# A third of a modulation product from TensorE matmuls to VectorE row products, and the latent heads' stage reordered

## The chip, the core and the metric

The kernel runs on one core of a Trainium2 chip. The metric is the time of one execution on the device in microseconds; the median of several runs is given. The core has five engines that run their own instruction streams and wait for each other through semaphores: TensorE (PE, matmuls into PSUM), VectorE (DVE), ScalarE (ACT), GpSimd (POOL) and SyncE (SP), which here only starts DMAs.

## What is computed

The reference applies two transformer blocks to 256 tokens of width 1024. The first one has stick-breaking attention and latent (MLA) attention side by side, an output projection, and an up projection, a convolution of three taps, a gate and a down projection. The second one begins with a modulation of its norms by a conditioning vector `c`:

```python
cond = jax.nn.silu(c)                       # (1, 1024)
mod = cond @ mod_w[l] + mod_b[l]            # mod_w: 1024 x 6144
sh1, sc1, g1, sh2, sc2, g2 = jnp.split(mod, 6, axis=-1)
h = _rmsnorm(x, norm1_g[l]) * (1 + sc1) + sh1
z = h @ w_in[l]
```

Everything is float32. `mod` depends on `c` and the weights alone, so the kernel may compute it at any time before the second block. Its first third (`sh1` and `sc1`, 2048 values) is the part that this change touches. The expert layer of the second block, which follows much later, reads most of the weights.

## The kernel before

All tiles have 128 partitions. Each engine has a function that issues its instructions in a fixed order (`tensor`, `scalar`, `vector`, `gpsimd`, `sync`), and every order is written out by hand; signals between the engines are named marks on semaphores. The instructions are recorded by helpers of one line each, so in the profile L107 is any matmul, L110 any transpose, L113 an activation, L116 a copy on ScalarE, L119 a table load, L125 a `tensor_tensor`, L133 a `scalar_tensor_tensor`, L136 a reciprocal.

The weights stream through a ring of seven slots of 2 MB. `STREAM` (line 51) gives the order of the loads and `PLACE` the slot of each; SP issues them in that order, each after the last use (`used`) of what lay in its slot, so a load that has to wait also holds up those behind it.

The modulation weights are twelve ring slots `modw` 0 to 11, four for each third of `mod`. `mod_slot(j)` multiplies one of them on TensorE: eight matmuls whose weights are 128x32 tiles of silu(c) with one column that isn't zero, and whose moving data are 512 columns of the modulation weights (each appears as two in the trace, x16). `mod_half` is half of that. `mod_sum` on VectorE copies the sums out of PSUM, `mod_total` turns them to a column per feature on TensorE and adds the bias on VectorE.

In the latent heads' stage (84 to 111 us) four pairs of heads, i = 0 to 3, go through `mla_scores(i)` on TensorE, `maxima` on VectorE, `shares` on ScalarE (Exp with sums) and on VectorE (division), `turn` on TensorE (six transposes), `turned` on ScalarE (copy out of PSUM), `values` on TensorE. TensorE's order puts `mod_slot` 0 to 5 and half of 6 in between. The same stage holds the root of the group norm for the stick-breaking heads (`column_sums(7, ...)`, `group_sums(0)`, a product for the total, `group_root(0)`, `group_factor(0)`, `group_norm(0..3)`), with the root near the end, and the rounding of the output projection's weights (`out_rounded`, `out_rest`) and inputs (`out_input`).

In the up projection each matmul operand of float32 is split in a high part (rounded by ScalarE, `up_rounded`) and a low part (what is left, by VectorE, or by GpSimd for the keys in `POOL_UP`: k = 3 and 7 of every block j from 1 on). Block j = 0 to 10 has one ring slot of weights and eight steps k with twelve matmuls of 256 columns; four weight buffers are used in turn, so the rounding of step n waits for the matmuls of step n - 4, and TensorE waits for the low part ahead of each step. The convolution, gelu and gating of block j - 1 are spread over the steps of block j (`conv_step`); GpSimd does the gated product and the low part of its result. The down projection does the same over 44 steps i with matmuls of 512 columns, all low parts of its weights on VectorE.

## Time and profile before

| | before |
|---|---|
| median of 3 runs | 939.18 us (938.42 to 939.66) |
| the profiled execution | 939.0 us, of which span 937.3 us |
| mean granted clock of TensorE | 0.937 of full speed |
| busy TensorE / VectorE / ScalarE / GpSimd | 84% / 37% / 33% / 13% of the span |
| DMA | 297.95 MB, mean 318 GB/s |

The profile shows one execution. A row of the timeline merges instructions that follow each other: start in us, time from the first start to the last end in us, engine, line, operation, output and inputs, forms, count, and in brackets the engine's idle time before it and what ended that. PEclk is the clock that TensorE was granted, as a share of full speed. Matmuls are pipelined, so successive groups overlap by a little.

### The profile page before, as it was taken

How to read it: one execution, taken by the hardware profiler on the slowest of the kernel's cores; microseconds unless marked ns; L12 is line 12 of the kernel's file. 1: busy time of each engine (PE TensorE's matmuls, PEld its weight loads, DVE VectorE, ACT ScalarE, POOL GpSimd, SP SyncE). 2: the span in 40 equal slices, each digit the busy share in tenths (PEclk: the TensorE clock that was granted, in tenths of full speed). 3: DMA queues.
4: the chain of work that ended last, by engine and by line, in shares of the span. 5: the costliest groups of instructions: out<-in, count | busy, mean ns of one | idle time of the engine just before them, and what ended most of it. 6: DMA issues, size and time to landing. Idle time of an engine off the chain costs nothing.

```text
span 937.3 us, 12394 instructions
## 1 busy us (share of the span) xinstructions
PE 790.7 (84%) x5204; PEld 524.5 (56%) x5204; DVE 349.4 (37%) x767; ACT 312.4 (33%) x623; POOL 125.7 (13%) x129
## 2 busy tenths in 40 slices
PE   9999999999999999999999998567666566755765
PEld 7985588999998867688786343123221222211213
DVE  6647766777776554399513110010100101001002
ACT  5756655766665476313633010001000000000002
POOL 0011032444441033100211000000000000000000
PEclk9999999999999999999999997988796998979868
DMA  9955917755535475735559999999999999999995
GB/s 357 407 188 216 430 66 299 293 187 189 189 132 186 180 261 199 282 134 191 214 229 408 429 429 427 427 429 426 429 428 428 429 426 430 425 428 430 427 427 208
DMA packets 24111, 297.95 MB, mean 318 GB/s; under 512 B 2672, under 2 KB 3056, under 8 KB 5488
## 3 DMA queue, kind: packets, MB, share of 16 engines
q1 hardware_dynamic: 24048, 297.09, 77.5%
q8 instruction: 43, 0.70, 0.3%
q14 instruction: 20, 0.16, 0.1%
HBM read 296.03 MB, written 1.05 MB: 317 GB/s over the span
## 4 chain that ended last, share of the span: by engine, by line
PE 57%; DMA 33%; ACT 4%; DVE 4%; issue 1%; POOL 0%; DVEq 0%; ACTq 0%; POOLq 0%
PE ps L107 57%; DMA ring<-in_exps 33%; ACT ar L113 1%; ACT ar L116 1%; ACT fr L116 1%; PE ps L110 1%; DVE ar L125 1%; ACT sq L113 0%; DVE fr L125 0%; DVE fr L133 0%; DVE misc L148 0%; DVE xg L133 0%; DVE yT L125 0%; DVE yT L133 0%; ACT L113 0%
## 5 line engine op out<-in xcount | busy, mean ns | idle before, releaser
L107 PE MATMUL ps<-ring,sq 128*32 128x512 f32 x944 | 139.7, 728 | 75.4 <-DMA ring<-in_exps 75.0
L107 PE MATMUL ps<-fr 128*128 128x256 f32 (+1 forms) x956 | 163.2, 323 | 1.9 <-ACT ar L116 1.4
L107 PEld LDWEIGHTS ps<-fr 128*128 128x128 f32 x956 | 140.1, 190 | 17.7 <-ACT ar L116 2.2
L107 PE MATMUL ps<-ring,ar 128*32 128x512 f32 (+3 forms) x792 | 102.4, 601 | 40.8 <-DMA ring<-in_exps 35.0
L107 PEld LDWEIGHTS ps<-ring,sq 128*32 128x32 f32 x944 | 29.1, 122 | 173.3 <-DMA ring<-in_exps 119.7
L125 DVE TENSOR_TENSOR ar<-ar,ps 128x512 f32<-128x512 f32 x9 | 6.2, 687 | 261.3 <-PE ps L107 261.3
L125 DVE TENSOR_TENSOR fr<-ring,fr 128x512 fp32r<-128x512 f32 (+1 forms) x96 | 77.9, 830 | 48.3 <-ACT fr L116 48.0
L116 ACT ACTIVATE ar<-ps 128x512 f32<-128x512 f32 (+4 forms) x48 | 27.2, 570 | 178.5 <-PE ps L110 145.5
L107 PEld LDWEIGHTS ps<-ring,ar 128*32 128x32 f32 (+1 forms) x792 | 27.1, 118 | 96.0 <-DMA ring<-in_exps 53.0
L107 PE MATMUL ps<-ar 128*128 128x512 f32 (+9 forms) x320 | 66.2, 427 | 11.0 <-DVE ar L125 9.3
L116 ACT ACTIVATE fr<-ring 128x512 fp32r<-128x512 f32 (+1 forms) x114 | 66.5, 623 | 25.6 <-PE ps L107 22.5
L107 PE MATMUL ps<-fr,fr_h 128*128 128x256 f32 x528 | 66.9, 283 | 0.0
L107 PEld LDWEIGHTS ps<-fr,fr_h 128*128 128x128 f32 x528 | 64.9, 191 | 0.0
L113 ACT ACTIVATE sq<-ps,misc 128x128 f32<-128x128 f32 x31 | 11.9, 456 | 158.1 <-PE ps L107 158.1
L125 DVE TENSOR_TENSOR ar<-ps,ar 128x512 f32<-128x512 f32 (+5 forms) x36 | 23.0, 659 | 110.6 <-PE ps L107 110.3
L107 PE MATMUL ps<-hT,ring 128*128 128x256 f32 (+1 forms) x288 | 64.0, 383 | 0.3 <-ACT hT L113 0.3
L107 PEld LDWEIGHTS ps<-ar 128*128 128x128 f32 (+4 forms) x320 | 36.3, 173 | 43.7 <-DVE ar L125 20.1
L107 PEld LDWEIGHTS ps<-hT,ring 128*128 128x128 f32 (+1 forms) x288 | 54.3, 190 | 9.8 <-issue 1.5
L125 POOL TENSOR_TENSOR ar<-ar 128x128 f32<-128x128 f32 (+2 forms) x21 | 11.2, 533 | 311.5 <-DVE ar L125 310.4
L113 ACT ACTIVATE ar<-ps 128x768 f32<-128x768 f32 (+1 forms) x21 | 15.0, 716 | 96.6 <-PE ps L107 89.4
L116 ACT ACTIVATE fr_h<-ring 128x512 fp32r<-128x512 f32 x66 | 40.2, 629 | 17.7 <-PE ps L107 17.7
L125 DVE TENSOR_TENSOR fr_h<-ring,fr_h 128x512 fp32r<-128x512 f32 x43 | 30.8, 716 | 25.8 <-ACT fr_h L116 25.8
(188 smaller groups left out, 929.7 us busy)
## 6 DMA issues: line engine op xcount, KB each, us to landing
ring<-in_exps SPq DMA_DIRECT2D x86, 2048.0 KB, 30.9
ring<-in_modw SPq DMA_DIRECT2D x12, 2048.0 KB, 8.8
ring<-in_wup SPq DMA_DIRECT2D x11, 2048.0 KB, 12.2
ring<-in_wdown SPq DMA_DIRECT2D x5, 2048.0 KB, 7.7
ar<-in_exps SPq DMA_DIRECT2D x5, 2048.0 KB, 13.0
ring<-in_win SPq DMA_DIRECT2D x4, 2048.0 KB, 8.2
ring<-in_exps SPq DMA_DIRECT2D x6, 1024.0 KB, 8.7
ring<-in_wo SPq DMA_DIRECT2D x2, 2048.0 KB, 9.7
```

The lines of the kernel that those rows point to most:

```text
L107: return Issue(self.e and self.e.matmul(o, l, r, start=start, stop=stop, skip_group_check=True))
L110: return Issue(self.e and self.e.transpose(o, i, ident))
L113: return Issue(self.e and self.e.activation(o, i, f, **kw))
L116: return Issue(self.e and self.e.activation(o, i, ACT.Copy, scale=scale))
L125: return Issue(self.e and self.e.tensor_tensor(o, a, b, op))
```

## The change

The first third of the modulation leaves TensorE and goes to VectorE. The host lays out `modw` 0 to 3 so that a partition holds a feature's column, 1024 long, and a slot holds 4 such tiles. `c` is loaded as a row into all partitions (`crow`, 512 KB), ScalarE takes its Silu after the first block of the up projection, and 16 instructions `tensor_tensor_reduce` on VectorE (`mod_column`) multiply 1024 elements by that row and sum them to one value of `mod` per partition: ten in the up projection (after the low part of k = 6 of blocks 1 to 10) and six in the down projection (ahead of the low parts of i = 5, 9, 13, 17, 21 and 25). The loads of `modw` 0 to 3 move to among those of the up projection's weights, and the slots of all loads around them change places.

In the latent heads' stage TensorE keeps `modw` 4, 5 and half of 6 between its steps. The root of the stick-breaking group goes from the end of the stage to its beginning, ahead of the first Exp on ScalarE, with a table load ahead of it and one behind it, and the group norms, the inputs and the rounded weights of the output projection are spread between the steps of the softmax.

```diff
-STREAM = ([("win", 1), ("win", 3), ("win", 2), ("wqkv", 0)] + [("modw", j) for j in range(7)] + [("wo", 0), ("wo", 1), ("wup", 0), ("modw", 7)]
-          + [("wup", j) for j in range(1, 11)] + [("wdown", j) for j in range(6)] + [("wple", 0), ("wgate", 0), ("wgate", 1)]
+STREAM = ([("win", 1), ("win", 3), ("win", 2), ("wqkv", 0)] + [("modw", 4), ("modw", 5), ("modw", 6), ("wo", 0), ("wo", 1), ("wup", 0), ("modw", 7)]
+          + [("wup", 1), ("modw", 0), ("wup", 2), ("wup", 3), ("wup", 4), ("modw", 1), ("wup", 5), ("wup", 6), ("wup", 7), ("wup", 8), ("modw", 2)]
+          + [("wup", 9), ("wup", 10), ("modw", 3)] + [("wdown", j) for j in range(6)] + [("wple", 0), ("wgate", 0), ("wgate", 1)]
...
+    def products_sum(self, o, a, b, total):
+        return Issue(self.e and self.e.tensor_tensor_reduce(out=o, in0=a, in1=b, scale=1.0, scalar=0.0, op0=ALU.mult, op1=ALU.add,
+                                                            accum_out=total))
...
             mla_scores(0)
-            mla_scores(1)
-            mod_slot(0, dve_lat["vm", 1])
-            mod_slot(1)
             pe.wait_ge(act_stick["o", 1])
             column_sums(7, [(tile(ar, k), act_stick["osq", k // 2]) for k in range(4)]).then_inc(pe_wo, "sums", 0)
+            mla_scores(1)
+            pe.wait_ge(act_wo["sums", 0])
+            pe.matmul(half(7, 1), ones, sd[:, 0, :], True, True).then_inc(pe_wo, "total", 0)
+            mod_slot(4, dve_lat["vm", 0])
             turn("mla", 0, mla_s[0])
-            mod_slot(2)
             mla_scores(2)
             turn("mla", 1, mla_s[1])
-            mod_slot(3)
-            pe.wait_ge(act_wo["sums", 0])
-            pe.matmul(half(7, 1), ones, sd[:, 0, :], True, True).then_inc(pe_wo, "total", 0)
+            mod_half(5, 0)
             mla_scores(3)
             values("mla", 0, mla_p[0], vm, dve_lat["vm", 1], dve_lat["qm", 3])
             values("mla", 1, mla_p[1], vm)
-            mod_slot(4, dve_lat["vm", 0])
+            mod_half(5, 1)
             turn("mla", 2, mla_s[0])
-            mod_slot(5)
+            mod_half(6, 0)
             turn("mla", 3, mla_s[1])
             values("mla", 2, mla_p[0], vm, act_wo["root", 0])
-            mod_half(6, 0)
             values("mla", 3, mla_p[1], vm)
-            mod_total(0)
...
+            act.tables("sqrt_and_others")
+            group_sums(0)
+            group_root(0)
+            act.tables("exp_and_others")
             shares("mla", 0, mla_s[0], scale)
             shares("mla", 1, mla_s[1], scale)
-            group_sums(0)
             turned("mla", 0, mla_p[0])
             turned("mla", 1, mla_p[1])
+            out_rounded(0, 0)
             shares("mla", 2, mla_s[0], scale)
+            out_input(0)
+            out_input(1)
             shares("mla", 3, mla_s[1], scale)
-            group_root(0)
             turned("mla", 2, mla_p[0])
+            out_input(2)
+            out_input(3)
+            out_rounded(0, 1)
             turned("mla", 3, mla_p[1])
...
+                if j == 0:
+                    act.wait_ge(landed["crow"]["all"])
+                    act.activation(sq[:, 0:1024], sq[:, 0:1024], ACT.Silu).then_inc(act_mod, "crow")
...
+            group_factor(0)
             maxima("mla", 2, mla_s[0], mla_mask, scale)
-            mod_sum(0)
+            for k in range(2):
+                group_norm(k)
             maxima("mla", 3, mla_s[1], mla_mask, scale)
             shares("mla", 2, mla_s[0])
+            for k in range(2, 4):
+                group_norm(k)
             shares("mla", 3, mla_s[1])
-            group_factor(0)
-            for k in range(4):
-                group_norm(k)
...
-            mod_total(0)
...
+            def mod_column(i):
+
+                j, o = i // 4, 1024 * (i % 4)
+                dve.wait_ge(loaded("modw", j), act_mod["crow"])
+                if i > 0:
+                    dve.wait_ge(dve_mod["column", i - 1])
+                t = dve.products_sum(sq[:, 1024:2048], slot("modw", j)[:, o:o + 1024], sq[:, 0:1024], mod[:, i:i + 1]).then_inc(dve_mod, "column", i)
+                if i == 15:
+                    dve.wait_ge(t)
+                    dve.tensor_tensor(mod[:, 0:16], mod[:, 0:16], col("mod_b", 0, 16), ALU.add).then_inc(dve_mod, "mod", 0)
+
+            DOWN_COLUMNS = (5, 9, 13, 17, 21, 25)
...
                     if j:
                         conv_step(j - 1, k)
+                    if j and k == 6:
+                        mod_column(j - 1)
...
+                if i in DOWN_COLUMNS:
+                    mod_column(10 + DOWN_COLUMNS.index(i))
                 dve.wait_ge(act_down["hi", f, n])
...
-                return (pe_mod["slot", j],)
+                return (dve_mod["column", 4 * j + 3] if j < 4 else pe_mod["slot", j],)
...
+                if (name, j) == ("wup", 2):
+                    sp.wait_ge(pe_joint["mix", "sums"])
+                    sp.dma_start(sq[:, 0:1024], A["crow"]).then_inc(landed["crow"], "all")
```

## Rows read from the trace of the kernel before

**Rows 1.** The page's part 4, the chain that ended last, by engine.

```profile
PE 57%; DMA 33%; ACT 4%; DVE 4%; issue 1%; POOL 0%; DVEq 0%; ACTq 0%; POOLq 0%
```

**Rows 2.** Windows: stretch and length, busy us of each engine, PEclk, DMA share, GB/s.

```profile
84.00:117.00 33.00, 31.30 (x246) 16.94 (x243) 23.85 (x55) 21.65 (x58) 1.28 (x1) 1.00 0.97 398
160.00:334.00 174.00, 174.00 (x1221) 163.84 (x1220) 114.08 (x192) 107.31 (x196) 60.88 (x42) 1.00 0.54 200
```

**Rows 3.** Timeline of TensorE in the latent heads' stage (columns as described above).

```profile
87.79 3.64 PE L107 MATMUL ps<-ring,ar 128*32 128x512 f32 x32
...
92.96 1.92 PE L107 MATMUL ps<-ring,ar 128*32 128x512 f32 x16
...
110.35 1.05 PE L107 MATMUL ps<-con,ar 128*128 128x4 f32 x8
111.26 2.11 PE L107 MATMUL ps<-fr 128*128 128x512 f32 x8
```

**Rows 4.** Timeline of ScalarE in the same stage.

```profile
85.71 0.63 ACT L113 ACTIVATE ar<-hT 128x512 f32<-128x512 f32 x1
88.90 0.40 ACT L113 ACTIVATE yT<-yT,misc 128x128 f32<-128x128 f32 x1 [2.56 <-DVE misc L129]
...
105.00 1.28 ACT L113 ACT_TABLE_LOAD   x1
...
107.84 0.81 ACT L116 ACTIVATE sq<-ps 128x768 f32<-128x768 f32 x1 [0.37 <-PE ps L110]
...
117.40 0.47 ACT L113 ACTIVATE sd<-ps,misc 128x256 f32<-128x256 f32 x1 [0.79 <-PE ps L107]
```

**Rows 5.** Timeline of VectorE in the same stage.

```profile
91.09 1.01 DVE L129 TENSOR_SCALAR yT<-yT,misc 128x128 f32<-128x128 f32 x4
...
96.43 0.96 DVE L125 TENSOR_TENSOR yT<-ps,yT 128x768 f32<-128x768 f32 x1 [2.31 <-PE ps L107]
...
106.81 1.75 DVE L136 RECIPROCAL rb<-sd 128x256 f32<-128x256 f32 x1 [0.57 <-ACT sd L113]
...
110.18 0.69 DVE L125 TENSOR_TENSOR fr<-ring,fr 128x512 fp32r<-128x512 f32 x1
```

**Rows 6.** Expert stage: a group of TensorE's timeline, and the window around it.

```profile
571.05 3.64 PE L107 MATMUL ps<-ring,ar 128*32 128x512 f32 x16 [2.97 <-DMA ring<-in_exps]
...
570.00:575.00 5.00, 3.64 (x16) 0.60 (x16) 0.24 (x1) 0.00 (x0) 0.00 (x0) 0.52 0.98 416
```

**Rows 7.** Timeline of VectorE, then of GpSimd, about one turn of the blocks.

```profile
177.97 0.68 DVE L125 TENSOR_TENSOR fr_h<-ring,fr_h 128x512 fp32r<-128x512 f32 x1
181.02 0.70 DVE L125 TENSOR_TENSOR fr<-ring,fr 128x512 fp32r<-128x512 f32 x1 [2.37 <-ACT fr L116]
181.65 1.77 DVE L125 TENSOR_TENSOR fr<-ring,fr 128x512 fp32r<-128x512 f32 x1
...
178.22 1.58 POOL L125 TENSOR_TENSOR yT<-yT 128x512 f32<-128x512 f32 x1 [3.27 <-DVE yT L133]
179.88 1.30 POOL L125 TENSOR_TENSOR fr_h<-ring,fr_h 128x512 fp32r<-128x512 f32 x1
181.26 1.62 POOL L125 TENSOR_TENSOR fr<-yT,fr 128x512 fp32r<-128x512 f32 x1
```

**Rows 8.** The same two engines at the end of the first block.

```profile
154.16 1.43 DVE L125 TENSOR_TENSOR fr_h<-ring,fr_h 128x512 fp32r<-128x512 f32 x1 [0.35 <-ACT fr_h L116]
...
153.75 1.29 POOL L125 TENSOR_TENSOR fr<-ring,fr 128x512 fp32r<-128x512 f32 x1 [12.63 <-ACT fr L116]
155.12 1.62 POOL L125 TENSOR_TENSOR fr_h<-ring,fr_h 128x512 fp32r<-128x512 f32 x1
```

**Rows 9.** Timeline of TensorE in the period of rows 7.

```profile
179.90 3.04 PE L107 MATMUL ps<-fr,fr_h 128*128 128x256 f32 x24
182.77 3.04 PE L107 MATMUL ps<-fr 128*128 128x256 f32 x24
```

**Rows 10.** The page's part 6, DMA issues: count, KB each, median us to landing.

```profile
ring<-in_wgate SPq DMA_DIRECT2D x2, 2048.0 KB, 7.6
```

More of the change, by code:

```diff
@@ L213, in build @@
         landed = {n: Signal(sem(f"{n}_in"), 16) for n in (
-            ["x0", "x2", "x4", "w0", "w1", "w2", "w4", "w6", "cols", "con", "rcount", "k4", "pos", "p", "brow"]
+            ["x0", "x2", "x4", "w0", "w1", "w2", "w4", "w6", "cols", "con", "rcount", "k4", "pos", "p", "brow", "crow"]
             + ["more3", "more6", "more7", "more8", "more9", "again17", "again18", "half0", "half1"])}
@@ L699, in tensor @@
                     if (j, n) == (0, 0):
-                        pe.wait_ge(dve_mod["mod", 0])
+                        pe.wait_ge(dve_lat["vm", 1])
                         column_sums(5, [(tile(sq, k), act_wo["osq", k // 2]) for k in range(4)]).then_inc(pe_wo, "sums", 1)
@@ L1266, in out_rounded @@
                 src, hi, _ = wo_part(n, k)
-                act.wait_ge(loaded("wo", n), pe_soft["mla", "scores", 3])
                 i = WO_ORDER.index((n, k))
+                act.wait_ge(loaded("wo", n), pe_soft["mla", "scores", 3] if i > 1 else pe_stick["values", 3])
                 if i > 7:
@@ L1293, in scalar @@
             scale = 96 ** -0.5
+            act.tables("sqrt_and_others")
+            group_sums(0)
+            group_root(0)
+            act.tables("exp_and_others")
             shares("mla", 0, mla_s[0], scale)
             shares("mla", 1, mla_s[1], scale)
-            group_sums(0)
             turned("mla", 0, mla_p[0])
             turned("mla", 1, mla_p[1])
+            out_rounded(0, 0)
             shares("mla", 2, mla_s[0], scale)
+            out_input(0)
+            out_input(1)
             shares("mla", 3, mla_s[1], scale)
-            group_root(0)
             turned("mla", 2, mla_p[0])
+            out_input(2)
+            out_input(3)
+            out_rounded(0, 1)
             turned("mla", 3, mla_p[1])
-            out_rounded(0, 0)
-            out_rounded(0, 1)
-            for k in range(4):
-                out_input(k)
-                if k == 1:
-                    mla_out(0)
-                elif k > 1:
-                    out_rounded(0, k)
+            out_rounded(0, 2)
+            out_rounded(0, 3)
+            mla_out(0)
             mla_out(1)
@@ L1734, in mod_sum @@
             def mod_sum(s):
-                dve.wait_ge(pe_mod["slot", 4 * s + 2], pe_mod["slot", 4 * s + 3], pe_mod["total", s - 1] if s else None)
+                dve.wait_ge(pe_mod["slot", 4 * s + 2], pe_mod["slot", 4 * s + 3], pe_mod["total", s - 1] if s > 1 else None)
                 dve.tensor_copy(ar[:, modp:modp + 512], bank(4 if s else 5)).then_inc(dve_mod, "sum", s)
@@ L1768, in vector @@
                 shares("mla", i, mla_s[i])
+            group_factor(0)
             maxima("mla", 2, mla_s[0], mla_mask, scale)
-            mod_sum(0)
+            for k in range(2):
+                group_norm(k)
             maxima("mla", 3, mla_s[1], mla_mask, scale)
             shares("mla", 2, mla_s[0])
+            for k in range(2, 4):
+                group_norm(k)
             shares("mla", 3, mla_s[1])
-            group_factor(0)
-            for k in range(4):
-                group_norm(k)
             out_rest(0, 0)
@@ L2280, in ring_load @@
                     return
-                if (name, j) == ("modw", 1):
+                if (name, j) == ("modw", 5):
                     sp.wait_ge(pe_in["q", 7])
@@ L2602, in lay_out @@
     A["wgate"] = _slots([L["w_ple_gate"][:, 0:512], L["w_ple_gate"][:, 512:1024]])
-    A["modw"] = np.stack([_rows(L["mod_w_2"][256 * t:256 * t + 256, 2048 * i:2048 * i + 2048]).reshape(128, SLOT)
-                          for i in range(3) for t in range(4)])
+    A["crow"] = np.broadcast_to(L["c_2"][0].reshape(1, 1024), (128, 1024))
+    w = L["mod_w_2"]
+    A["modw"] = np.stack([w[:, 512 * t:512 * t + 512].reshape(1024, 4, 128).transpose(2, 1, 0).reshape(128, SLOT) for t in range(4)]
+                         + [_rows(w[256 * t:256 * t + 256, 2048 * i:2048 * i + 2048]).reshape(128, SLOT) for i in range(1, 3) for t in range(4)])
     w = L["w_in_2"]
```

## The prediction

> **What bounds the kernel now.** I read the chain that ended last first: TensorE carries 57% of it, and almost all the rest (33%) is waiting for DMA [rows 1], in order of time the expert weights of the last 370 us. The windows then give two different stages around the change. From 84 to 117 us (scores and softmax of the latent heads) TensorE has work nearly always (31.30 us of 33), but much of that work is filler: modulation products that stand between steps of a chain from TensorE to VectorE to ScalarE and back [rows 2]. From 160 us to 334 us (up and down projections) TensorE is busy without a gap, 174.00 of 174.00 us, at a granted clock of 1.00 (2.4 GHz) [rows 2]. The filler in the first stage can go without loss; in the second stage anything that makes TensorE wait is paid in full. The DMA tail starts when compute frees ring slots, so a shift of everything ahead of it should arrive at the end one to one, in either direction.
>
> **Part 1: what leaves TensorE.** Slots 0 to 3 of the modulation weights and one turning product go. On TensorE slots 0 and 1 took 3.64 us together, slot 2 1.92 and slot 3 the same, the turning 1.05 [rows 3]: 8.4 us of queue in 23.5 us (87.8 to 111.3). If TensorE were the bound there, 8.4 us would be gained; if the softmax chain were, nothing. So the chain has to be followed.
>
> Before, ScalarE's square ends at 86.3, its first Exp starts at 88.90, and it ends the last turned copy at 108.65 [rows 4]. After the change it first does the root of the stick-breaking group: a table load (1.28, as the one at 105.00), the copy of the sums, a wait for the total, the root (0.47), and a table load back (1.28) [rows 4]. With the third and fourth product of TensorE in between (sums 0.6, scores 1.4, total 0.7) the root ends near 89.7 and the first Exp starts near 91.0: the chain starts 2.1 us later. From there I add the same durations in the new order. Two pairs' Exps, 1.86 each, end at 94.7; the factors of the first pair (VectorE, reciprocal 0.17 and four products 1.01, [rows 5]) are ready at 94.1, its transposes and the turned copy end at 95.8, the third scores at 97.4, where the maxima that wait for them began at 96.43 before [rows 5]. VectorE meanwhile does the group's reciprocal, 1.75 [rows 5], until 97.7; third maxima to 100.0, two norms, fourth maxima from 100.85 to 103.1, about where they were before, Exps to 105.0, factors to 106.35, transposes to 107.3, turned copy to 108.2, values to 109.1. The output products start there instead of at 111.26 [rows 3]: 2.2 us earlier. ScalarE's queue then holds two roundings, the two head outputs, four roundings and the sums: they end at 114.2 instead of 116.6 (2.4 earlier); the second root now has a table load ahead of it, mostly under the total, and ends at 115.9 instead of 117.9 (2.0 earlier), and the low parts that VectorE makes from 119.7 on follow it. **I take 2.2 us gained**; the other 6.2 us of removed products become waits. The two ends are 0 (a wait in my chain missed) and 8.4.
>
> TensorE will idle for about 3 us near 91 to 94. In the expert stage a pause of 2.97 us was followed by a granted clock of 0.52, and 16 products took 3.64 us there instead of 1.92 [rows 6]; other pauses of the same length left the clock at 1.00. If it falls in the latent stage it costs up to about 2 us of the gain.
>
> **Part 2: what VectorE takes up.** Sixteen products with sums, each 128x1024 in and out. No row shows this operation. Products of 512 elements took 0.69 us and of 768 took 0.96 [rows 5], so a kilo-element at the same rate takes 0.96 + 256 x 1.05 ns = 1.23 us. Ends: 1.23 us if the sum is free, about 2.3 us if each element takes twice as long. Sixteen are 20 us of VectorE, which is busy for 114 of 174 us in the two projections [rows 2], so there is room in total. What matters is where they stand.
>
> In each of j = 1 to 10 the column comes after the low part of k = 6. In the period that I read, this low part runs from 177.97 to 178.65, then VectorE is idle for 2.37 us until 181.02 [rows 7]. By VectorE's own queue a column of 1.23 us fits. But GpSimd works in just that gap: the gated product (178.22, 1.58 us), the low part of k = 7 (179.88, 1.30, to 181.18), the low part of the product (181.26, 1.62) [rows 7]. And the two engines keep each other out when both read two operands of SBUF. VectorE's low part at 181.65 took 1.77 us instead of 0.69: it ended 0.54 after GpSimd's instruction of 181.26 did. GpSimd's at 181.26 took 1.62 instead of 1.30, being behind VectorE's of 181.02. The pair at 154.16 and 155.12 shows who is next: VectorE, waiting for GpSimd's 153.75 to end at 155.04, got in ahead of GpSimd's next one, which took 1.62, 0.33 more than alone [rows 8]. The Trainium skill says the same in "SBUF — State Buffer", section "Who interferes with whom": a VectorE instruction with two SBUF inputs and a GpSimd one that reads SBUF exclude each other for the whole instruction. The rows above agree with it.
>
> So the column, issued at about 178.6 behind GpSimd's gated product, will start when that ends (179.8), ahead of the low part of k = 7. That one is then held for 0.33 us (what a VectorE product of 512 cost it) plus 512 more elements, 0.53: 0.86 us. When does TensorE need it? The group of 24 products for k = 6 and 7 starts at 179.90 and the next at 182.77 [rows 9], so k = 7 starts at 181.34, only 0.16 us after 181.18. Part of that is the signal's way between the engines; I take 0.10 us of cover. **Each column stalls TensorE by about 0.76 us, ten times 7.6 us.** It doesn't add up within a period (the low parts of the next block's k = 0 and 1, done at 182.6 and 184.3, are needed at 183.5 and 185.0), nor is it made up for, since each period hangs on TensorE's own progress. If GpSimd got in first the column would start at 181.2 and hold back GpSimd's next one, and with it the low part of k = 0, for a stall of a little over 1 us instead: no order is free.
>
> In the down projection the six columns have no GpSimd work that TensorE needs soon (its last two instructions are wanted at f = 20). A low part is made as soon as a buffer is free, three steps of 1.36 us ahead of its use less 1.4 us of rounding: 2.7 us of cover against a column of 1.23. I take 0; if the cover were gone it would be 1.2 us a column.
>
> **Part 3: ScalarE, ring and queues.** The Silu over 1024 elements costs about 1.0 us (a copy of 768 took 0.81) and a table load 1.28 [rows 4]. It stands ahead of the rounding of (1, 0), whose low part is ready 2.4 us before its use; so 1.3 us of delay is hidden: 0. The row of c goes behind slot 2 of the up weights on SP's queue, which waits for the second half of modulation slot 6; half a megabyte behind two lands some 8 us later, ahead of the Silu. The tightest load is the last up slot: it waits for column 7 (j = 8, k = 6), about 0.9 us after TensorE begins that k; it is wanted a period later, 11.7 us on. Loads of 2 MB with nothing ahead of them landed in 7.6 us [rows 10], and nothing is ahead here: 4 us of cover, so I take 0. Modulation slot 3 and the first down slot stand behind it, 5 us each, and have 3.5 us of cover.
>
> **Sum.** 10 x 0.76 - 2.2 = +5.4 us on the profiled execution (939.0 us, span 937.3), which stands 0.2 under the median of 939.18: 944.6.
>
> **Rivals.** (a) The columns are hidden: the sum form doesn't hold GpSimd back, or TensorE's cover is larger than read. For it: 2.37 us of idle VectorE each period. Against it: [rows 8]. Then only the latent stage counts: 939.2 - 2.2 = 937.0, between 934.5 and 939. Chance 0.20, of it 0.12 beyond the bound of change. (b) The product with sum runs at half rate. Then the lock is held 1.07 us longer, 10 x 1.83 = 18.3, less 2.2: 955.3. This is the far slow side, decided by the duration of one instruction, from about 1.5 us upward. Chance 0.12. The Trainium skill, "Vector Engine (DVE) Microarchitecture Reference", "Points that are easy to get wrong", says a scalar_tensor_tensor with two 32-bit SBUF sources has half the rate with accumulation; no run here shows one yet. (c) The latent stage gives back 5 to 8 us, because the order by hand shortens waits I count as fixed; with the stalls this gives 936.5 to 942, say 939. Chance 0.12, of it 0.05 faster. (d) The forecast, with 0.5 to 1.1 us a column and 0 to 4 us of gain, a fallen clock or a late slot included: 941.2 to 949. Chance 0.56.
>
> A measurement of this kernel can tell 0.2% (1.9 us) from no change. Faster: 0.12 + 0.05 = 0.17. Same: 0.08 + 0.07 = 0.15. Slower: 0.56 + 0.12 = 0.68. The range leaves out (b) and the lower part of (a): 936.5 to 950.
>
> **What would show it.** Right: in each of ten periods a VectorE instruction of 128x1024 that starts inside a GpSimd instruction and is stretched, GpSimd's low part into fr_h at about 2.1 us instead of 1.30, and TensorE waiting some 0.8 us for it; periods of 12.3 us instead of 11.5; six columns of 1.23 us in the down projection with no wait of TensorE; output products beginning near 109 with a pause near 91 to 94. Wrong: periods of 11.5 us (rival a), columns of over 2 us there (b), output products starting before 106 (c), TensorE waiting for the ring in the up projection.

## The result and the profile after

The changed kernel takes 949.74 us (median of 4 runs, 948.91 to 949.97) against 938.80 us (4 runs, 938.31 to 939.66) for the one before on the same chip: 1.0113 of its time, 95% interval 1.0098 to 1.0128. It is **10.9 us slower**. I had forecast slower, with 944.6 us (5.4 us over the profiled run) and a range of 936.5 to 950. The profiled execution of after took 949.59 us, span 947.9, mean granted clock 0.938; that of before 939.0, 937.3 and 0.937.

The page of after first: its part 4 (the chain that ended last, by engine), and two groups of its part 5 (form, count, busy time and mean ns, idle time before and what ended it).

```profile
PE 46%; DMA 33%; DVE 9%; ACT 6%; POOL 4%; issue 1%; SPq 0%; POOLq 0%; DVEq 0%; ACTq 0%
...
L108 PE MATMUL ps<-fr 128*128 128x256 f32 (+1 forms) x956 | 163.2, 323 | 1.6 <-ACT ar L117 1.4
...
L108 PE MATMUL ps<-fr,fr_h 128*128 128x256 f32 x528 | 69.5, 285 | 8.3 <-POOL fr_h L126 8.3
```

Against [rows 1] TensorE has fallen from 57% of the chain to 46%, GpSimd has come from 0 to 4%, VectorE from 4 to 9%. The last row says where: TensorE waits 8.3 us for `fr_h`, the low parts that GpSimd makes.

The same events in both timelines show how the difference grows (starts in us):

| event | before | after | difference |
|---|---|---|---|
| last product ahead of the latent stage (four matmuls behind a ScalarE copy) | 79.95 | 79.29 | -0.66 |
| first transpose behind the output projection | 136.42 | 135.83 | -0.59 |
| up projection, k = 0 of j = 1 | 159.72 | 159.13 | -0.59 |
| first step of the down projection | 274.85 | 285.18 | +10.33 |
| work behind the down projection | 334.72 | 345.05 | +10.33 |
| end of the span | 937.3 | 947.9 | +10.6 |

The first 0.66 us lies ahead of everything that TensorE does differently; in the traces of all kernels of this document that event starts anywhere from 78.86 to 79.97. The latent heads' stage, the work of part 1, comes to +0.07 us where I had -2.2. The ten blocks of the up projection cost **10.92 us** where I had 7.6; the down projection costs nothing, as forecast.

**One period of the up projection**, j = 2, read as [rows 7] and [rows 9]: timelines of VectorE, GpSimd and TensorE of after (start, length, instruction, idle time before it).

```profile
178.21 0.68 DVE L126 TENSOR_TENSOR fr_h<-ring,fr_h 128x512 fp32r<-128x512 f32 x1
178.81 1.22 DVE L156 CUSTOM_DVE_ANT_0 sq<-ring,sq 128x1024 f32<-128x1024 f32 x1
179.96 0.08 DVE L156 DVE_READ_ACCUMULATOR2_ANT misc<- 128x1 f32 x1
...
178.46 2.72 POOL L126 TENSOR_TENSOR yT<-yT 128x512 f32<-128x512 f32 x1 [3.25 <-DVE yT L134]
181.26 1.28 POOL L126 TENSOR_TENSOR fr_h<-ring,fr_h 128x512 fp32r<-128x512 f32 x1
182.61 1.63 POOL L126 TENSOR_TENSOR fr<-yT,fr 128x512 fp32r<-128x512 f32 x1
...
180.13 1.60 PE L108 MATMUL ps<-fr,fr_h 128*128 128x256 f32 x12
182.59 1.70 PE L108 MATMUL ps<-fr,fr_h 128*128 128x256 f32 x12 [0.85 <-POOL fr_h L126]
184.13 3.04 PE L108 MATMUL ps<-fr 128*128 128x256 f32 x24
```

The column (the instruction CUSTOM_DVE_ANT_0 of L156) takes 1.22 us and is not stretched. What is stretched is GpSimd's gated product: 2.72 us against 1.58 in [rows 7], 1.14 more, nearly the whole column. Its next instruction, the low part of k = 7, has its normal 1.28 us but ends 1.13 us later against TensorE's k = 6 than before, and TensorE waits 0.85 us. The steps of k = 6 and k = 7, one group of 24 products before, are now two of 12, and from k = 6 to the next k = 0 it takes 4.00 us (180.13 to 184.13) instead of 2.87. The next period's k = 6 starts at 192.77, 12.64 us later; before, a period was 11.51. All blocks j = 2 to 10 look so (gated product 2.71 or 2.72 us nine times).

In the first period, j = 1, it goes another way (VectorE, GpSimd, TensorE again):

```profile
166.46 2.32 DVE L156 CUSTOM_DVE_ANT_0 sq<-ring,sq 128x1024 f32<-128x1024 f32 x1
...
166.10 1.60 POOL L126 TENSOR_TENSOR yT<-yT 128x512 f32<-128x512 f32 x1 [3.26 <-DVE yT L134]
167.77 2.14 POOL L126 TENSOR_TENSOR fr_h<-ring,fr_h 128x512 fp32r<-128x512 f32 x1
...
167.77 1.60 PE L108 MATMUL ps<-fr,fr_h 128*128 128x256 f32 x12
169.96 1.69 PE L108 MATMUL ps<-fr,fr_h 128*128 128x256 f32 x12 [0.60 <-POOL fr_h L126]
```

Here the column is the one that is held (2.32 us), and it gets in between GpSimd's two instructions, so that the low part takes 2.14 instead of 1.30. That is the picture that I had forecast for all ten, and it costs 12.36 - 11.51 = 0.85 us. With nine of 1.12 to 1.13 that makes the 10.9.

**The latent heads' stage**: TensorE's timeline and the windows (stretch, length, busy us of each engine, granted clock, DMA share, GB/s) of after.

```profile
93.40 1.54 PE L111 MATMUL ps<-con,yT 128*128 128x128 f32 x6 [3.14 <-DVE yT L130]
95.84 2.93 PE L108 MATMUL ps<-ar 96*128 96x128 f32 x8 [0.90 <-ACT ar L117]
98.56 1.49 PE L111 MATMUL ps<-con,yT 128*128 128x128 f32 x6
...
110.67 3.02 PE L108 MATMUL ps<-fr 128*128 128x512 f32 x12
...
94.00:97.00 3.00, 2.10 (x9) 1.61 (x8) 2.72 (x6) 0.81 (x1) 0.00 (x0) 0.50 0.92 393
97.00:100.00 3.00, 3.00 (x16) 2.29 (x14) 1.16 (x2) 0.00 (x0) 0.00 (x0) 0.50 0.01 5
100.00:104.00 4.00, 4.00 (x33) 2.45 (x32) 3.07 (x7) 3.69 (x12) 0.00 (x0) 0.97 0.02 4
```

TensorE idles for 3.14 us behind its filler, and the granted clock is 0.50 (1.2 GHz) in all six microseconds after that: the first transposes take 1.54 us, the third scores 2.93. On the full clock these two take 0.88 and 1.58 us (a row of d2 and one of c1, below). The output projection begins at 110.67.

### The profile page after: what moved, and what is told of

The parts are those of the page before. It is cut to its first block, busy times and chain, and to the rows that moved or that the text cites. A ratio compares the mean times of both kernels' runs of the same rounds, so it can differ in the third digit from the quotient of the medians.

```text
span 947.9 us, 12289 instructions
## 1 busy us (share of the span) xinstructions
PE 783.5 (83%) x5132; PEld 522.7 (55%) x5132; DVE 368.5 (39%) x798; ACT 317.3 (33%) x627; POOL 137.2 (14%) x129
## 4 chain that ended last, share of the span: by engine, by line
PE 46%; DMA 33%; DVE 9%; ACT 6%; POOL 4%; issue 1%; SPq 0%; POOLq 0%; DVEq 0%; ACTq 0%
PE ps L108 45%; DMA ring<-in_exps 32%; DVE yT L134 4%; POOL yT L126 3%; DVE fr L126 2%; POOL fr_h L126 1%; ACT yT L114 1%; ACT ar L114 1%; ACT ar L117 1%; ACT fr L117 1%; DVE fr_h L126 1%; DVE ar L126 1%; DMA ring<-in_win 1%; PE ps L111 1%; ACT fr_h L117 1%
## 5 line engine op out<-in xcount | busy, mean ns | idle before, releaser
L108 PE MATMUL ps<-ring,sq 128*32 128x512 f32 x944 | 136.4, 713 | 78.7 <-DMA ring<-in_exps 78.3
L108 PE MATMUL ps<-ring,ar 128*32 128x512 f32 (+3 forms) x728 | 96.2, 609 | 42.1 <-DMA ring<-in_exps 36.9
L108 PE MATMUL ps<-fr,fr_h 128*128 128x256 f32 x528 | 69.5, 285 | 8.3 <-POOL fr_h L126 8.3
L108 PEld LDWEIGHTS ps<-ar,yT 128*128 128x128 f32 x256 | 32.0, 199 | 15.7 <-issue 14.5
```

The costliest lines, as they stand in the source:

```text
L108: return Issue(self.e and self.e.matmul(o, l, r, start=start, stop=stop, skip_group_check=True))
```

## The experiments

My theory after this reading: (1) all of the loss is the columns of the up projection, because VectorE and GpSimd exclude each other; (2) the gain of the latent stage is there, but the granted clock takes it back. The rival of (1) was a cost of each column that has nothing to do with GpSimd (a fixed price of the new instruction, or its place in VectorE's queue). The rival of (2) was that moving the root ahead of the first Exp costs what the removed products give.

### The columns taken away: a1

```diff
-                t = dve.products_sum(sq[:, 1024:2048], slot("modw", j)[:, o:o + 1024], sq[:, 0:1024], mod[:, i:i + 1]).then_inc(dve_mod, "column", i)
+                t = dve.memset(small[:, 0:1], 0.0).then_inc(dve_mod, "column", i)
...
-                    dve.tensor_tensor(mod[:, 0:16], mod[:, 0:16], col("mod_b", 0, 16), ALU.add).then_inc(dve_mod, "mod", 0)
+                    dve.tensor_copy(mod[:, 0:16], col("mod_b", 0, 16)).then_inc(dve_mod, "mod", 0)
```

> The changed kernel with the sixteen products with sums left out (a memset of one element stands in each one's place, so the signals that free the ring slots stay; the first third of the modulation is then only its bias). Loads, Silu, the order of the latent stage and everything else as in the changed kernel. Theory L (the columns lock GpSimd out of its reads, and nothing else of them costs): periods of the up projection back to 11.51 us from 12.63, so 11.0 us less than the changed kernel: 938.7 us, that is level with the kernel before, since the latent stage gained nothing. Rival W (part of the 11 us is from the loads in their new order, the Silu or the ring): some periods stay longer than 11.51 and the time lies above 940.

Measured: 938.33 us (10 runs), 0.9995 of before (0.9983 to 1.0007; before on this chip 938.39). The whole loss goes with the columns, and what is left of the change (the ring, the row of c, the Silu and the latent stage together) is worth nothing that can be measured: 1.6 us less to 0.7 us more by the interval.

### The columns in another place: a2

```diff
-                    if j and k == 6:
+                    if j and k == 1:
                         mod_column(j - 1)
```

> The same ten columns, each after the low part of k = 1 instead of k = 6. There VectorE has 1.12 us of idle time and GpSimd has nothing until about 2.2 us later. Theory L: VectorE does the same work, but GpSimd's low part of k = 7 is in time again: periods of 11.5 to 11.6 us, 939 us in all (938.5 to 940.5). Rival V (the columns cost because VectorE's queue is too full, so its own low parts come late): the low part of k = 2, which has only some 0.4 us of cover, comes 0.1 us late at most by VectorE's rows, but if V holds the periods stay at 12.3 or more, 947 to 950 us.

Measured: 938.70 us (10 runs), 0.9998 (0.9985 to 1.0010). The window of the up projection, VectorE's column with the low part behind it, and GpSimd's instruction ahead of it, in the trace of a2:

```profile
160.00:285.00 125.00, 125.00 (x1006) 123.37 (x1005) 99.19 (x176) 81.65 (x153) 58.13 (x40) 1.00 0.53 217
...
183.83 1.21 DVE L156 CUSTOM_DVE_ANT_0 sq<-ring,sq 128x1024 f32<-128x1024 f32 x1
184.98 0.08 DVE L156 DVE_READ_ACCUMULATOR2_ANT misc<- 128x1 f32 x1
185.03 0.69 DVE L126 TENSOR_TENSOR fr_h<-ring,fr_h 128x512 fp32r<-128x512 f32 x1
...
181.74 1.62 POOL L126 TENSOR_TENSOR fr<-yT,fr 128x512 fp32r<-128x512 f32 x1
```

All sixteen columns are done, and TensorE is busy for 125.00 of 125.00 us again. GpSimd has just ended when the column starts (its last instruction runs from 181.74 to 183.36, its next one starts at 185.66). So the work itself has no price; its place had one. This is also rival (a) of the prediction, had the change put the columns here.

### Half the length: a3

```diff
-                t = dve.products_sum(sq[:, 1024:2048], slot("modw", j)[:, o:o + 1024], sq[:, 0:1024], mod[:, i:i + 1]).then_inc(dve_mod, "column", i)
+                t = dve.products_sum(sq[:, 1024:1536], slot("modw", j)[:, o:o + 512], sq[:, 0:512], mod[:, i:i + 1]).then_inc(dve_mod, "column", i)
```

> The sixteen products over 512 instead of 1024 elements, in the places of the changed kernel (half of each sum is left out). Theory L with the order seen in the trace (the column goes ahead of GpSimd's gated product and holds it for its whole length): the hold falls by 512 elements of 1.04 ns, from 1.14 to 0.61 us, and the period from 12.63 to 12.10: 5.3 us less over ten periods, 944.4 us. If the stall had a fixed part per instruction (a queue or a drain), the period would stay above 12.3 and the time above 946.5.

Measured: 945.26 us (5 runs), 1.0064 (1.0040 to 1.0088), 6.9 us over before. VectorE and GpSimd in j = 2 of a3:

```profile
178.53 0.68 DVE L156 CUSTOM_DVE_ANT_0 sq<-ring,sq 128x512 f32<-128x512 f32 x1
...
178.18 2.18 POOL L126 TENSOR_TENSOR yT<-yT 128x512 f32<-128x512 f32 x1 [3.27 <-DVE yT L134]
```

The gated product is 0.60 us longer than in [rows 7], against 1.14 with the full column, and the period is 12.11 us, 0.60 over before. Both times that is 0.08 us less than the column takes, 0.68 and 1.22. So the price follows the length of the column (0.53 us less a period for 0.54 us less of column), and no fixed part shows. The first period goes its own way here too: GpSimd's gated product goes first, and j = 1 is only 0.33 us over before (168.01 to 179.85, 11.84 us). With nine of 0.60 that makes 5.7 us, which is what the trace has for the ten blocks (120.80 us from 159.37 to 280.17, 115.13 before); the rest to the 6.9 measured lies within the interval (4 to 8 us).

### One of the two inputs in PSUM: a4

The Silu's row is copied to two banks of PSUM that are free during the up projection, and the ten columns there read it from PSUM; place and length stay. TensorE waits for the last of them before it uses these banks, in the down projection.

```diff
+                        act.copy(ps[:, 6:8, :].rearrange("p b t -> p (b t)"), sq[:, 0:1024]).then_inc(act_mod, "crow")
...
+                row = ps[:, 6:8, :].rearrange("p b t -> p (b t)") if i < 10 else sq[:, 0:1024]
+                t = dve.products_sum(sq[:, 1024:2048], slot("modw", j)[:, o:o + 1024], row, mod[:, i:i + 1]).then_inc(dve_mod, "column", i)
```

> Columns at k = 6 as in the changed kernel and as long, but for the ten in the up projection the row of silu(c) is copied once to two free banks of PSUM and read there, so each has one input in SBUF. Theory L (two inputs in SBUF take what GpSimd reads through): GpSimd's gated product takes 1.6 us instead of 2.72, periods of 11.5 us, 939 us (938.5 to 940). Rival P (any long VectorE instruction in that gap delays GpSimd, by its write to SBUF or by the signals): periods stay at 12.3 to 12.6, 947 to 950.

Measured: 938.57 us (10 runs), 1.0002 (0.9987 to 1.0016). VectorE and GpSimd in j = 2 of a4:

```profile
177.81 1.21 DVE L156 CUSTOM_DVE_ANT_0 sq<-ring,ps 128x1024 f32<-128x1024 f32 x1
...
177.46 1.59 POOL L126 TENSOR_TENSOR yT<-yT 128x512 f32<-128x512 f32 x1 [3.26 <-DVE yT L134]
```

The same instruction at the same point, 1.21 us long, now lies beside the gated product, and the latter takes 1.59 us as before. This is the run that decides: what costs is that the column reads both its operands from SBUF while GpSimd reads there too, and neither its length, its place nor its write to SBUF by themselves. GpSimd's product had two inputs in SBUF in every run, so whether one would do wasn't tried. Theory (1) is shown.

### The latent stage with more filler: b2 and b3

From here on the columns stand behind k = 1. b2 puts modulation slot 5 right behind slot 4 in the long pause; b3 repeats slot 4 there.

In b2:

```diff
             mod_slot(4, dve_lat["vm", 0])
+            mod_slot(5)
             turn("mla", 0, mla_s[0])
...
-            mod_half(5, 0)
...
-            mod_half(5, 1)
```

In b3:

```diff
             mod_slot(4, dve_lat["vm", 0])
+            mod_slot(4)
             turn("mla", 0, mla_s[0])
```

> Columns after k = 1 and, in the latent stage, all of modulation slot 5 right behind slot 4, ahead of the first transposes, where TensorE waited 3.1 us in the changed kernel. Same instructions as with the columns after k = 1 alone. Theory C (the pause makes the granted clock fall to 0.5 from about 94 to 101 us, and that costs the 2.2 us which the new order should have gained): the pause shrinks to 1.3 us, the clock stays at 1.00, third scores take 1.6 us instead of 2.9, the output products start some 2 us earlier, 936.5 us. Rival O (the new order itself gains nothing): clock at 1.00, but the products start as late, 938.5.

> Columns after k = 1, and modulation slot 4 multiplied twice in a row (the second time starts the sum anew, so the result stays): 1.9 us of work that serves only to fill the pause; slot 5 stays where it was. Theory C: although TensorE has 1.9 us more to do, the kernel gets faster, as with slot 5 moved: 936.5 to 937. Rival O: 938.5 or slower.

Measured: b2 938.80 us (12 runs), 0.9992 (0.9980 to 1.0003); b3 939.18 us (12 runs), 0.9989 (0.9973 to 1.0006); before on this chip 938.64 (the ratios aren't those of the medians). The expected gain did not come as a median. But the runs of b3 fall in two groups: four at 934.70, 934.85, 934.85 and 935.71 us, eight from 937.87 to 941.47. Those of b2 are spread from 935.54 to 939.93. The profiled execution of b3 was one of the long ones:

```profile
94.07 0.88 PE L111 MATMUL ps<-con,yT 128*128 128x128 f32 x6 [1.42 <-DVE yT L130]
95.85 2.93 PE L108 MATMUL ps<-ar 96*128 96x128 f32 x8 [0.90 <-ACT ar L117]
...
92.00:96.00 4.00, 1.68 (x15) 0.79 (x7) 2.60 (x11) 3.33 (x13) 0.00 (x0) 0.97 0.63 143
96.00:100.00 4.00, 4.00 (x17) 3.20 (x17) 2.58 (x3) 0.00 (x0) 0.00 (x0) 0.50 0.90 381
```

The pause of 3.14 us has become 1.42 and 0.90, and still the clock is at 0.50 from 96 to 100. So the filler was too little for the clock to hold in this execution. That it held in the four short ones is an inference, since only one execution has a trace, but the mean granted clock of each run speaks for it: 0.938 to 0.940 in the four short runs, 0.928 to 0.935 in the eight long ones, and 0.940 and 0.941 in the two shortest of b2 (0.929 to 0.935 in the others). It is a mean over the whole kernel and doesn't say where the clock fell, and in the runs of before (937.47 to 940.96 us) it varies from 0.931 to 0.945 too, so it is a sign and no proof. The medians of the two groups of b3 (934.85 and 939.53) are 4.7 us apart, more than the stage costs in the traces (57.00 us in this one, 53.88 in d2, measured as below); where the rest comes from no run shows.

### The old order without the removed products: c0

ScalarE, VectorE and TensorE go through the stage as before the change; slots 0 to 3 and the turning product are just gone.

> Columns after k = 1, and the latent stage in the order of the kernel before on all three engines, with modulation slots 0 to 3 and the turning product simply gone: slots 4, 5 and half of 6 where they were. The first Exp is 2 us earlier than in the changed kernel, but TensorE now waits over 4 us ahead of the first transposes. Theory C: the clock falls there too (about 92 to 99 us) and takes back what the shorter queue gives: 937.5 to 938.7. If the clock doesn't fall or doesn't matter: 936.5 or less.

Measured: 939.38 us (10 runs), 1.0006 (0.9997 to 1.0016). TensorE and two windows of c0:

```profile
91.72 1.54 PE L111 MATMUL ps<-con,yT 128*128 128x128 f32 x6 [3.73 <-DVE yT L130]
...
111.26 2.13 PE L108 MATMUL ps<-fr 128*128 128x512 f32 x7 [0.41 <-DVE fr L126]
...
92.00:96.00 4.00, 3.10 (x12) 2.52 (x12) 1.19 (x5) 1.51 (x4) 0.00 (x0) 0.50 0.00 0
96.00:100.00 4.00, 3.56 (x16) 2.84 (x15) 2.14 (x4) 1.44 (x4) 0.00 (x0) 0.71 0.00 0
```

Without a product between the scores and the first transposes the pause is 3.73 us and the clock falls to 0.50 too. 8.4 us of TensorE's work are gone and nothing is gained. The stage comes out the same with the reordering and without it, and in both the clock falls. So the 0 of the latent stage isn't a gain that the reordering ate up.

### The old order with its fillers moved: c1

All engines again go in the order of before. Slots 4 and 5 go into the first pause (where slots 0 and 1 had been), half of slot 6 behind the first transposes. The diff is against c0.

```diff
             mla_scores(0)
             mla_scores(1)
+            mod_slot(4, dve_lat["vm", 0])
+            mod_slot(5)
             pe.wait_ge(act_stick["o", 1])
             column_sums(7, [(tile(ar, k), act_stick["osq", k // 2]) for k in range(4)]).then_inc(pe_wo, "sums", 0)
             turn("mla", 0, mla_s[0])
+            mod_half(6, 0)
             mla_scores(2)
...
-            mod_slot(4, dve_lat["vm", 0])
             turn("mla", 2, mla_s[0])
-            mod_slot(5)
             turn("mla", 3, mla_s[1])
             values("mla", 2, mla_p[0], vm, act_wo["root", 0])
-            mod_half(6, 0)
```

> The same, with slots 4 and 5 in the first pause and the half of 6 behind the first transposes. Theory C: clock at 1.00 through the stage; third scores about 0.8 us earlier and fourth 1.9 us earlier than in the kernel before, then the root and reciprocal of the stick-breaking group are late next; output products about 2 us earlier: 936.5. Against the slot 5 run it shows whether moving the root to the front was worth anything: if the two are level, it was not.

Measured: **936.15 us** (7 runs, 935.65 to 937.35), 0.9972 (0.9962 to 0.9983) of before (938.64 on this chip). This is a gain over before and over the changed kernel. Three windows and three groups of TensorE of c1:

```profile
92.00:96.00 4.00, 3.98 (x29) 2.82 (x30) 1.75 (x6) 1.75 (x6) 0.00 (x0) 1.00 0.99 422
96.00:100.00 4.00, 3.53 (x27) 2.37 (x25) 2.97 (x7) 2.67 (x9) 0.00 (x0) 1.00 1.01 430
...
104.00:108.00 4.00, 4.00 (x22) 2.98 (x22) 3.46 (x6) 3.60 (x8) 0.00 (x0) 0.50 0.00 0
...
93.83 1.58 PE L108 MATMUL ps<-ar 96*128 96x128 f32 x8
...
101.97 1.27 PE L111 MATMUL ps<-con,yT 128*128 128x128 f32 x6 [1.93 <-DVE yT L130]
...
108.28 2.81 PE L108 MATMUL ps<-fr 128*128 128x512 f32 x8
```

The clock stays at 1.00 until 100, and the third scores take 1.58 us. The price is a later pause (1.93 us before the third transposes) and a clock of 0.50 there.

### Both orders with the clock kept: d2 and d1

d2 is the new order with one and a half times slot 4 more than needed, the halves of slots 5 and 6 each one place earlier, and two groups of two matmuls whose result nobody reads. d1 is c1 with four and two such matmuls ahead of the third and fourth transposes. The diff is that of d2.

```diff
-            mod_slot(4, dve_lat["vm", 0])
+            pe.wait_ge(dve_lat["vm", 0])
+            mod_half(4, 0)
+            mod_slot(4)
+            mod_slot(4)
             turn("mla", 0, mla_s[0])
+            mod_half(5, 0)
             mla_scores(2)
             turn("mla", 1, mla_s[1])
-            mod_half(5, 0)
+            mod_half(5, 1)
...
-            mod_half(5, 1)
-            turn("mla", 2, mla_s[0])
             mod_half(6, 0)
+            for _ in range(2):
+                pe.matmul(half(5, 0), ones, con[:, 0:256], True, True)
+            turn("mla", 2, mla_s[0])
+            for _ in range(2):
+                pe.matmul(half(5, 0), ones, con[:, 0:256], True, True)
             turn("mla", 3, mla_s[1])
```

> The new order of the latent stage, columns after k = 1, and TensorE's waits filled nearly to the brim: slot 4 two and a half times ahead of the first transposes (the last pass gives the right sums), half of slot 5 behind them, products that nobody reads ahead of the third and fourth transposes. Theory C, after the runs with 1.9 us of filling fell in two groups near 934.8 and 939.4: with no pause above about 0.5 us until 104 us the granted clock stays at 1.00 in every execution and all fall in the lower group, 934.8 to 935.5. Rival G (the two groups have another cause, such as where ScalarE or DMA stand): a median of 937 to 939 with the same two groups.

> The old order with slots 4 and 5 in the first pause, and products that nobody reads (1.9 and 0.9 us) ahead of the third and fourth transposes, where the clock still fell to 0.5 in the profile of that kernel (102 to 108 us). Theory C: clock at 1.00 in the whole stage, 0.5 to 1 us less than the 936.15 of that kernel: 935.3. Rival: the chain from the root of the group norm to the inputs of the output projection sets the end there, so the clock of TensorE no longer matters: 936.1.

Measured: d2 935.99 us (8 runs, 934.73 to 936.55), 0.9974 (0.9963 to 0.9985); d1 **935.65 us** (9 runs, 934.72 to 936.73), 0.9972 (0.9962 to 0.9981); before on this chip 938.39. Windows and TensorE of d2, then two windows of d1:

```profile
92.00:96.00 4.00, 3.43 (x26) 1.95 (x23) 3.43 (x10) 2.22 (x8) 0.00 (x0) 1.00 0.66 205
96.00:100.00 4.00, 4.00 (x30) 2.40 (x30) 3.72 (x8) 2.71 (x9) 0.00 (x0) 1.00 1.04 381
...
92.97 0.88 PE L111 MATMUL ps<-con,yT 128*128 128x128 f32 x6 [0.57 <-DVE yT L130]
...
107.54 3.03 PE L108 MATMUL ps<-fr 128*128 128x512 f32 x12
...
104.00:108.00 4.00, 2.77 (x23) 1.68 (x22) 3.60 (x6) 3.97 (x9) 0.00 (x0) 1.00 0.00 0
108.00:112.00 4.00, 3.19 (x8) 2.48 (x9) 4.00 (x8) 3.97 (x9) 1.90 (x1) 0.61 0.00 0
```

Neither kernel's runs fall in two groups now. In d2 the clock stays at 1.00 through the stage, in d1 until 108. Measured from the last product ahead of the stage to the first transpose behind the output projection (the two events of the table above), the traces give:

| kernel | from | to | length | against before |
|---|---|---|---|---|
| before | 79.95 | 136.42 | 56.47 | |
| after | 79.29 | 135.83 | 56.54 | +0.07 |
| c0, old order, products gone | 79.51 | 136.45 | 56.94 | +0.47 |
| c1, old order, fillers moved | 79.82 | 134.14 | 54.32 | -2.15 |
| d1, the same, clock kept longer | 79.68 | 134.02 | 54.34 | -2.13 |
| d2, new order, clock kept | 78.86 | 132.74 | 53.88 | -2.59 |

a1 to a4, whose latent stage is that of after, come to +0.17 to +0.54 in the same measure, b2 and b3 (both traces are of long executions) to +0.66 and +0.53.

The new order with its clock kept gives 2.6 us in the trace and 2.4 us in the medians (935.99 against 938.39), where I had forecast 2.2. The old order gives as much with its fillers moved (2.1 in the trace, 2.7 and 2.5 in the medians of d1 and c1). So the root moved ahead of the Exp, with its two table loads, is worth nothing that these runs can measure. The work that left TensorE is worth 2.1 to 2.7 us if the clock is kept at least until 100, and nothing if it isn't. That d1 isn't measurably faster than c1, though its clock falls only after 108, fits the rival of its expectation, that the late fall in c1 lies beside another chain: in both the total for the second root starts at the same distance behind the first event (114.39 - 79.82 and 114.25 - 79.68, both 34.57).

## Why the prediction was right in its direction and short in its size

**What bounds the kernel: right.** The sum had 7.6 us of stalls less 2.2 us of gain, 5.4; the traces have 10.92 and +0.07. Both terms were mis-sized, and in the same direction. TensorE in the up projection had no slack, and a shift there arrived at the end: +10.33 at the start of the down projection, +10.6 at the end of the span. In the latent stage the filler could go, but not "without loss": it was what kept the clock up.

**Part 2, the mechanism: right. Its size: 7.6 against 10.92 us.** The duration of the column was right (1.23 forecast, 1.22 measured, and 0.08 for reading the accumulator, which I had not counted and which delays nobody). That VectorE and GpSimd exclude each other over it was right, and a4 shows it. The term that was mis-sized is the stall of 0.76 us, and its step is "issued behind GpSimd's gated product, will start when that ends (179.8), ahead of the low part of k = 7". That happened in j = 1 alone. In the nine others the column went ahead of the gated product. [rows 7] hold the hint, which I passed over: the gated product of 178.22 began while VectorE's low part ran to 178.65, and took 1.58 us where a product of that size takes 1.30. So at 178.65 it had not been running, as I took it, but waiting. The trace of after bears this out: from the end of VectorE's instruction to its own end the gated product took 1.15 us in [rows 7] (178.65 to 179.80) and 1.15 us again in j = 2 of after (180.03 to 181.18). The column, issued back to back, took its turn. It then held GpSimd for its whole length, 1.14 us, and not only for 0.86.

Even the sentence that "no order is free" had the right number in the wrong place: I gave a little over 1 us to another order (the column only behind the low part of k = 7), and 1.12 us is what the order with VectorE first costs. That the numbers meet is chance.

The second part of the gap is what a restart costs. In j = 1 the forecast held to the hundredth up to TensorE: low part held for 0.86 us (1.28 behind k = 6 in [rows 7] and [rows 9], 2.14 now), k = 7 begun at 2.19 us instead of 1.44, 0.75 late. But the next k = 0 is 0.86 us late (171.50 - 167.77 = 3.73 against 2.87), since twelve products that start after a wait take 0.1 us more than in a stream (1.54 us to the next group against 1.44). With 0.86 once and 1.12 nine times the sum is 10.9: of the missing 3.3 us the order makes up 9 x 0.26 = 2.3 and the restart ten times 0.1.

The Trainium skill's "SBUF — State Buffer", section "Who interferes with whom", which the prediction named, states the exclusion that after and a4 show: with one input in PSUM the gated product took 1.59 us, with both in SBUF 2.72.

**Part 1: the chain right, the time not.** The forecast of ScalarE's chain held: the first Exp, which I had near 91.0, starts at 90.23 in a run that is 0.66 us ahead, so 0.1 us from the forecast. TensorE's pause was there, and of the length I named (3.14 for "about 3"). What failed is the weight of the last sentence of that part. I had seen that such a pause can be followed by a granted clock of about a half, and priced it at "up to about 2 us of the gain", but I left it out of the sum. It happened in every trace with a pause of 1.42 to 3.73 us ahead of the first transposes: after and a1 to a4 had 0.50 from 97 to 100, b2 and b3 from 96 to 100, c0 from 92 to 96. Where that pause is 0.29 us (before, c1, d1) or 0.57 us (d2), the clock is at 1.00 from 92 to 100. Its price was the whole gain: -2.2 forecast, +0.07 measured, -2.59 when the clock was kept. I had set [rows 6] against other pauses of the expert stage that left the clock alone, as if the two were alike in number. The trace of before has 21 pauses of 2.96 to 2.98 us ahead of such a group of 16 products. In four of them the products took 1.92 us, in the other 17 they took 2.84 to 3.64, so the rows at hand had spoken for putting the fallen clock into the sum. Two of the 21 that follow each other:

```profile
595.73 1.92 PE L107 MATMUL ps<-ring,sq 128*32 128x512 f32 x16 [2.97 <-DMA ring<-in_exps]
600.62 3.36 PE L107 MATMUL ps<-ring,sq 128*32 128x512 f32 x16 [2.97 <-DMA ring<-in_exps]
```

**The down projection and part 3: right.** From 285.18 to 345.05 it is 59.87 us, and 274.85 to 334.72 before is the same; six columns of 1.21 to 1.22 us hide. ScalarE's Silu came at 155.62, a quarter microsecond of it a wait for the row of c, which I had said would be there ahead of it:

```profile
154.08 1.28 ACT L114 ACT_TABLE_LOAD   x1
155.62 1.06 ACT L114 ACTIVATE sq<-sq 128x1024 f32<-128x1024 f32 x1 [0.25 <-DMA sq<-in_crow]
```

That too is hidden: the difference in the table stays at -0.59 up to the first column. TensorE waits for the ring nowhere in the up projection (its idle time there is 8.3 us, all for `fr_h`).

**The rivals.** (a), hidden columns, is what a2 and a4 made of the kernel, at 938.7 and 938.6 us (I had 937.0, the latent gain included that isn't there without the clock); the change as it is has them where they don't hide. (b), half rate, fell with one row: 1.22 us for 1024 elements. The Trainium skill's "Vector Engine (DVE) Microarchitecture Reference", "Points that are easy to get wrong", says that a scalar_tensor_tensor with two SBUF sources that aren't bf16 has half the throughput, with no read port left for the accumulator. No run here has that instruction with a sum; this `tensor_tensor_reduce` with two float32 sources in SBUF ran at the full rate of a product. (c), 5 to 8 us from the latent stage, fell: with the clock kept it gives at most 2.6 in the traces and 2.7 in the medians. The forecast (d) had 0.5 to 1.1 us a column and 0 to 4 us of gain; both terms came out at the bad edge together, 1.09 and none. Those two edges add up to 11 us or 950.2, not to the 949 that I gave as the end of (d).

**Luck.** That 949.74 lies inside the range of 936.5 to 950 is in part luck. The upper end was set to leave (b) out, not from the terms, and 10.9 us on top of the 939.18 that I had reckoned from would be 950.1; before came out at 938.80 in the comparison.

## What to carry to other kernels

Before an instruction with two SBUF inputs is put into VectorE's idle time, lay GpSimd's timeline beside it: ten columns of 1.2 us cost 10.9 us behind k = 6, and nothing behind k = 1, where GpSimd was idle, nor behind k = 6 with one input in PSUM. An instruction on GpSimd that shows 1.58 us where its kind takes 1.30 is already waiting for VectorE, and what VectorE issued back to back went ahead of it in nine of ten periods. Filler between the steps of a chain isn't dead weight: whoever takes it out should look at the granted clock of the windows behind each pause, and keep enough to hold it. Removing 8.4 us of work gave nothing (c0, 939.38 us); with three of the fillers that were left moved into the pauses the same kernel was 2.5 us faster than before (c1). And where a trace has many pauses of one length, all of them should be counted before their effect is put at nothing.

## What the runs showed of the hardware that I had not expected

- A GpSimd instruction that waits for VectorE's two-input instruction to end mostly did not get its turn then when VectorE had the next one ready: in nine of ten periods of after, and nine of ten of a3, the gated product waited through two VectorE instructions. In j = 1 of both kernels it got in between them, although the starts stand alike (low part, gated product 0.25 us later, column 0.61 after the low part, in j = 1 and in j = 2). What decides this is open. The first column is the first instruction of its kind in the program and the only one that doesn't wait for a column ahead of it; neither was tried.
- A product with sum over 1024 float32 elements takes 1.21 to 1.22 us, over 512 0.68 us, the same as a plain product of that size (0.68), and 0.08 us more for reading the accumulator.
- The granted clock fell to 0.50 (1.2 GHz) after pauses of 1.42 and 0.90 us with 0.87 or 0.88 us of transposes between them, in the traces of b2 and b3, and the twelve runs of b3 fall in two groups (934.70 to 935.71, and 937.87 to 941.47). In a chain of short steps from engine to engine a clock of 0.50 for some 6 us went with a stage that was 2.66 us longer (56.54 in after, 53.88 in d2).
- The first group of twelve matmuls after a wait of 0.33 us (a3) to 0.85 us (after) took 1.54 us to the next group's start, in the stream 1.44.
